# Query and key chunks turned by VectorE in 32x32 blocks instead of by TensorE, with tokens ordered by remainder modulo 4

## The reference, cut to what matters

```python
proj = x @ w_in                       # (256, 2048) @ (2048, 19456)
q_a, k_a, v_a, q_r, k_r, v_r, g_r, gate_a, gate_b = split(proj)
# A: 3 groups x 8 heads of 128, (window, dilation) = (128,1), (512,4), (2048,16)
#    rotary on the first 32 of 128 columns of q_a and k_a
#    query t attends to t, t-d, t-2d, ... inside the window; groups mixed by their softmax sums
# B: retention, 8 heads, qk width 128, v width 256, rotary on all 128 columns,
#    decay per head, norm per head, swish gate g_r
y = (sigmoid(gate_a) * (o_a @ w_branch_attn) + sigmoid(gate_b) * (o_r @ w_branch_ret)) @ w_out
x = layer_norm(alpha * x + y)
# 32 experts in 4 groups: top group, then top 2 SwiGLU experts of it (2048 -> 512 -> 2048)
x = layer_norm(alpha * x + moe(x))
```

## Time and profile before

| | us |
|---|---|
| median of 3 runs (2060.63 to 2063.73) | 2062.45 |
| profiled execution, span from first to last instruction | 2058.1 |
| PE busy / DVE busy / ACT busy in the span | 1766.7 / 994.9 / 757.1 |

### The profile page before, as it was taken

How to read it: one execution, slowest core, us unless ns; L and a number is a source line. 1 busy time by engine, 2 the same in 40 slices (tenths; PEclk the granted TensorE clock), 3 DMA queues, 4 the chain that set the end, 5 groups by cost and what they waited for, 6 DMA issues and landing times.

```text
span 2058.1 us, 25311 instructions
## 1 busy us (share of the span) xinstructions
PE 1766.7 (86%) x9868; PEld 1141.9 (55%) x9868; DVE 994.9 (48%) x1469; ACT 757.1 (37%) x1321; POOL 15.3 (1%) x34
## 2 busy tenths in 40 slices
PE   9999999999999999999999986666566666666667
PEld 7888888888888888888888541111112111111222
DVE  5454454555444444566565564334433433343357
ACT  5444444344444444354443422222222222222221
POOL 0000000000000000000000000000000000000000
PEclk9999999999999999999999988887888888887888
DMA  7556655455556555467677999999999999999998
GB/s 247 194 175 189 199 175 176 150 184 187 191 181 194 172 185 178 155 188 238 218 279 287 381 428 425 429 431 429 427 430 433 430 426 429 431 430 427 430 428 367
DMA packets 139042, 615.07 MB, mean 299 GB/s; under 512 B 14228, under 2 KB 14900, under 8 KB 117840
## 3 DMA queue, kind: packets, MB, share of 16 engines
q1 hardware_dynamic: 138240, 611.75, 77.5%
q0 software_dynamic: 720, 2.18, 0.6%
HBM read 609.61 MB, written 2.36 MB: 297 GB/s over the span
## 4 chain that ended last, share of the span: by engine, by line
PE 54%; DMA 33%; issue 10%; DVE 2%; ACT 0%; SPq 0%; DVEq 0%; POOL 0%; POOLq 0%
DMA W<-in_w_expert_up_dram 21%; PE PS L593 14%; PE PS L595 14%; PE PS L594 14%; DMA W<-in_w_expert_down_dram 11%; PE PS L1173 5%; PE PS L1224 2%; PE PS L962 1%; PE PS L1314 0%; PE PS L1129 0%; DVE ZACC L2234 0%; PE PS L1052 0%; DMA VC<-VS 0%; PE PS L1295 0%; PE PS L939 0%
## 5 line engine op out<-in xcount | busy, mean ns | idle before, releaser
L570 DVE TENSOR_TENSOR WL<-RAW,WH 128x1024 fp32r<-128x1024 f32 x384 | 457.4, 1221 | 403.9 <-ACT WH L566 402.5
L566 ACT ACTIVATE WH<-RAW 128x1024 fp32r<-128x1024 f32 x384 | 394.5, 1058 | 261.6 <-PE PS L595 199.8
L593 PE MATMUL PS<-WH,XH 128*128 128x512 f32 x1216 | 480.0, 395 | 0.1
L595 PE MATMUL PS<-WH,XL 128*128 128x512 f32 x1216 | 474.0, 390 | 0.0
L594 PE MATMUL PS<-WL,XH 128*128 128x512 f32 x1216 | 473.3, 389 | 0.0
L1173 PE MATMUL PS<-W,XE 128*32 128x512 f32 x2016 | 277.3, 698 | 135.0 <-DMA W<-in_w_expert_up_dram 133.6
L2234 DVE TENSOR_TENSOR ZACC<-PS,ZACC 128x1024 f32<-128x1024 f32 x124 | 146.0, 1219 | 294.3 <-PE PS L1295 294.3
L1224 PE MATMUL PS<-W,HT 128*32 128x512 f32 x992 | 171.0, 851 | 135.7 <-DMA W<-in_w_expert_down_dram 135.7
L593 PEld LDWEIGHTS PS<-WH,XH 128*128 128x128 f32 x1216 | 228.3, 188 | 49.3 <-issue 1.7
L595 PEld LDWEIGHTS PS<-WH,XL 128*128 128x128 f32 x1216 | 228.2, 188 | 48.3
L594 PEld LDWEIGHTS PS<-WL,XH 128*128 128x128 f32 x1216 | 228.6, 188 | 45.8
(11 more groups left out here) (333 smaller groups left out, 1472.7 us busy)
## 6 DMA issues: line engine op xcount, KB each, us to landing
RAW<-in_w_in_dram SPq DMA_DIRECT2D x304, 512.0 KB, 4.5
W<-in_w_expert_gate_dram SPq DMA_DIRECT2D x61, 2048.0 KB, 28.6
W<-in_w_expert_up_dram SPq DMA_DIRECT2D x61, 2048.0 KB, 33.0
W<-in_w_expert_down_dram SPq DMA_DIRECT2D x28, 4096.0 KB, 35.2
RAW<-in_w_branch_ret_dram SPq DMA_DIRECT2D x32, 512.0 KB, 5.2
RAW<-in_w_out_dram SPq DMA_DIRECT2D x32, 512.0 KB, 6.0
W<-in_w_expert_down_dram SPq DMA_DIRECT2D x7, 2048.0 KB, 30.4
RAW<-in_w_branch_attn_dram SPq DMA_DIRECT2D x16, 512.0 KB, 5.3
```

Source lines behind the costliest of these rows:

```text
L566: act.activation(WH[:, i % RING], RAW[:, i % RING], ACT.Copy).then_inc(hi_done, 1)
L570: dve.tensor_tensor(WL[:, i % RING], RAW[:, i % RING], WH[:, i % RING].bitcast(F32), ALU.subtract).then_inc(lo_done, 1)
L593: pe.matmul(PS[:, bank + t], hs, wh, start=first and j == 0, stop=False)
L595: mm = pe.matmul(PS[:, bank + t], ls, wh, start=False, stop=end)
```

## The change

Query and key chunks are no longer transposed by PE and read by ACT. DVE transposes NAT itself: for each of the four groups of 32 partitions of NAT (a) and each of the four groups of 32 head columns (b) one instruction turns 32 partitions by 256 elements (2 token tiles x 4 heads x 32 columns) straight into QT, KTT, QRT or KRT; 16 instructions a chunk, four at each of the steps READ+2 to READ+5 (q_a, k_a) or READ+4 to READ+7 (q_r, k_r). The group of four waits for a drain and, in the second half, for scores long done. ACT reads the next chunk into NAT when the 16 are done.

So that a group of 32 partitions holds the tokens of one remainder modulo 4, tokens stand in a tile in the order given by `turn`: high_x and low_x write XH and XL permuted, positions are loaded by four DMAs, one for each remainder, the masks, decays and triangle are permuted on the host, and read_turn (heads alone) and read_merged put the order right again. QT of group 0 and KRT are laid out with the heads innermost, so that DVE writes them with a distance of 4 and of 8 elements, and PE loads weights from them with the same distances. move_values issues four DMAs of 64 KB where it issued one of 256 KB.

```diff
 LAG = 2
-V_MOVES = (NG - 1) * TOK
...
 RET_AT = [123 + 5 * h for h in range(HH)]
-EARLY_ROTS = [c for c in ROTS if CHUNKS[c][0] in ("qa", "ka")]
-TURNS = sorted([(READ[c] + 3 + (0 if c in EARLY_ROTS else 3 * t), "chunk", c, t) for c in ROTS for t in range(TOK)]
-               + [(ATT_AT[h] + 13, "head", h, 0) for h in range(HH)])
+TURNS = [(ATT_AT[h] + 13, h) for h in range(HH)]
 NT = len(TURNS)
...
     t = np.arange(P)
+    turn = CLASSES * (t % ROWS) + t // ROWS
...
         q = CLASSES * (t[:, None] % CM) + member
         for g, (window, dilation) in enumerate(GROUPS):
-            k = np.arange(SEQ)[None, :] if g == 0 else CLASSES * np.arange(CM)[None, :] + member
+            k = np.concatenate([turn, P + turn])[None, :] if g == 0 else CLASSES * np.arange(CM)[None, :] + member
...
             col += ok.shape[1]
     first[:, C_ID:C_ID + P] = np.eye(P)
-    first[:, C_TRI:C_TRI + P] = t[:, None] <= t[None, :]
...
-    n = (np.arange(TOK)[None, :] * P + t[:, None]).astype(np.float64)
+    n = (np.arange(TOK)[None, :] * P + turn[:, None]).astype(np.float64)
...
+    QT = at("QT", 96, [NG, QD, HH, TOK, ROWS])
+    KTT = at("KTT", 108, [NG, QD, HH, TOK, ROWS])
...
-    KRT = at("KRT", 136, [HH, SEQ])
+    QRT = at("QRT", 132, [QD, HH, TOK, ROWS])
+    KRT = at("KRT", 136, [QD, HH, TOK, ROWS])
     VR = at("VR", 140, [2, TOK, CH])
...
-                            sp.dma_start(POSI[:], positions.rearrange("b (t p) -> p (b t)", p=P),
-                                         allow_slow_non_contiguous=True).then_inc(pos_landed, 16)
+                            for r in range(CLASSES):
+                                sp.dma_start(POSI[r * ROWS:(r + 1) * ROWS],
+                                             positions.rearrange("b (t m r) -> r m (b t)", m=ROWS, r=CLASSES)[r],
...
                 pe.wait_ge(sums_read, half * NP + PLAIN.index(c) + 2)
+        q_near = QT[:, 0].rearrange("p a h t m -> p (a h t m)").rearrange("p (n h) -> p n h", h=HH)
+        k_ret = KRT[:].rearrange("p a h t m -> p (a h t m)").rearrange("p (n t h) -> p n t h", t=TOK, h=HH)
+
         def att_scores(half, h):
-            pe.wait_ge(turn_read, half * NT + turn_index("chunk", 2 * NG - 1, 1) + 2)
+            pe.wait_ge(qk_turned, len(ATT_ROTS) * (half + 1))
             if h:
                 pe.wait_ge(o_norm, half * HH + h)
             for u in range(TOK):
-                pe.matmul(PS[:, S0 + u, 0:SEQ], QT[:, 0, h, u * P:(u + 1) * P], KTT[:, 0, h], start=True, stop=True)
+                pe.matmul(PS[:, S0 + u, 0:SEQ], q_near[:, TOK * u * CM:TOK * (u + 1) * CM, h],
+                          KTT[:, 0, :, h].rearrange("p a t m -> p t a m"), start=True, stop=True)
             for u in range(TOK):
                 for g in range(1, NG):
                     c0 = SEQ + (g - 1) * CM
                     for c in range(P // CM):
-                        own = slice(u * P + c * CM, u * P + (c + 1) * CM)
-                        mm = pe.matmul(PS[c * CM:(c + 1) * CM, S0 + u, c0:c0 + CM], QT[:, g, h, own], KTT[:, g, h, own],
+                        r = P // CM * u + c
+                        mm = pe.matmul(PS[c * CM:(c + 1) * CM, S0 + u, c0:c0 + CM], QT[:, g, r, h], KTT[:, g, r, h],
                                        start=True, stop=True)
             mm.then_inc(scored, 1)
...
             if h == 0:
                 pe.wait_ge(o_norm, half * HH + HH)
             else:
                 pe.wait_ge(r_masked, half * HH + h)
-            pe.matmul(PS[:, S0, 0:SEQ], KRT[:, h, 0:P], QRT[:, h, :], start=True, stop=True)
-            pe.matmul(PS[:, S0, SEQ:SEQ + P], KRT[:, h, P:SEQ], QRT[:, h, P:SEQ], start=True,
+            pe.matmul(PS[:, S0, 0:SEQ], k_ret[:, :, 0, h], QRT[:, :, h].rearrange("p a t m -> p t a m"),
+                      start=True, stop=True)
+            pe.matmul(PS[:, S0, SEQ:SEQ + P], k_ret[:, :, 1, h], QRT[:, :, h, 1], start=True,
                       stop=True).then_inc(r_scored, 1)
         def ret_values(half, h):
...
-            bank = turn_bank(kind, a, t)
-            pe.wait_ge(turn_read, half * NT + n + (0 if bank == S0 else 1))
-            if bank == S0 and half:
-                pe.wait_ge(r_masked, HH)
-            if kind == "chunk":
-                pe.wait_ge(rotated, half * len(ROTS) + ROTS.index(a) + 1)
-                for h in range(HH):
-                    mm = pe.transpose(PS[:, bank, h * P:(h + 1) * P], NAT[:, t, h * DH:(h + 1) * DH], ident)
-            else:
-                pe.wait_ge(o_norm, half * HH + a + 1)
-                for u in range(TOK):
-                    mm = pe.transpose(PS[:, TB, u * P:(u + 1) * P], ON[:, u], ident)
+        def turn(half, h):
+            pe.wait_ge(turn_read, half * HH + h)
+            pe.wait_ge(o_norm, half * HH + h + 1)
+            for u in range(TOK):
+                mm = pe.transpose(PS[:, TB, u * P:(u + 1) * P], ON[:, u], ident)
             mm.then_inc(turned, 1)
         for half in range(2):
...
         def high_x(b):
             act.wait_ge(x_turned, b + 1)
-            act.activation(XH[:, 2 * b:2 * b + 2].rearrange("p k n -> p (k n)"), PS[:, 2 + b % X_BANKS],
+            act.activation(XH[:, 2 * b:2 * b + 2].rearrange("p k (t r m) -> p (k t) r m", r=CLASSES, m=ROWS),
+                           PS[:, 2 + b % X_BANKS].rearrange("p (x m r) -> p x r m", m=ROWS, r=CLASSES),
                            ACT.Copy).then_inc(x_high, 1)
...
                 if before and before[-1] in ROTS:
-                    act.wait_ge(turned, half * NT + turn_index("chunk", before[-1], 1) + 1)
+                    if before[-1] in ATT_ROTS:
+                        act.wait_ge(qk_turned, half * len(ATT_ROTS) + ATT_ROTS.index(before[-1]) + 1)
+                    else:
+                        act.wait_ge(r_turned_in, half * len(RET_ROTS) + RET_ROTS.index(before[-1]) + 1)
                 elif before:
                     act.wait_ge(g_used, half * len(GRS) + GRS.index(before[-1]) + 1)
                 if kind == "gr":
...
                                scale=0.5).then_inc(sums_read, 1)
-        def read_turn(half, n, kind, a, t):
-            act.wait_ge(turned, half * NT + n + 1)
-            if kind == "head":
-                dst = OT[:, half * HH + a].rearrange("p (m r) -> p r m", r=CLASSES)
-                src = PS[:, TB, 0:SEQ].rearrange("p (r m) -> p r m", r=CLASSES)
-            else:
-                kd, g, _, _ = CHUNKS[a]
-                buf = {"qa": QT[:, g], "ka": KTT[:, g], "qr": QRT, "kr": KRT}[kd]
-                dst = buf[:, :, t * P:(t + 1) * P]
-                src = PS[:, turn_bank(kind, a, t)].rearrange("p (h n) -> p h n", h=HH)
-                if kd == "qa" or (kd == "ka" and g):
-                    part = P // CLASSES
-                    dst = buf.rearrange("p h (r m) -> p h r m", r=CLASSES)[:, :, :, t * part:(t + 1) * part]
-                    src = PS[:, turn_bank(kind, a, t)].rearrange("p (h m r) -> p h r m", h=HH, r=CLASSES)
-            act.activation(dst, src, ACT.Copy).then_inc(turn_read, 1)
+        def read_turn(half, h):
+            act.wait_ge(turned, half * HH + h + 1)
+            act.activation(OT[:, half * HH + h].rearrange("p (t r m) -> p r t m", r=CLASSES, m=ROWS),
+                           PS[:, TB, 0:SEQ].rearrange("p (r t m) -> p r t m", r=CLASSES, m=ROWS),
+                           ACT.Copy).then_inc(turn_read, 1)
         def att_exp(half, h):
             act.wait_ge(masked, half * HH + h + 1)
...
         def read_merged(j, t):
             act.wait_ge(m_turned, TOK * j + t + 1)
-            act.activation(MT[:, 4 * j:4 * j + 4, t * P:(t + 1) * P],
-                           PS[:, S0 + t].rearrange("p (b n) -> p b n", b=4),
+            act.activation(MT[:, 4 * j:4 * j + 4, t * P:(t + 1) * P].rearrange("p b (m r) -> p b r m", r=CLASSES),
+                           PS[:, S0 + t].rearrange("p (b r m) -> p b r m", b=4, r=CLASSES),
                            ACT.Copy, scale=0.5).then_inc(m_read, 1)
         def merged_high(q):
...
         def low_x(b):
             dve.wait_ge(x_high, b + 1)
-            dve.tensor_tensor(XL[:, 2 * b:2 * b + 2].rearrange("p k n -> p (k n)"), PS[:, 2 + b % X_BANKS],
-                              XH[:, 2 * b:2 * b + 2].rearrange("p k n -> p (k n)").bitcast(F32),
-                              ALU.subtract).then_inc(x_low, 1)
+            low, high = (s[:, 2 * b:2 * b + 2].rearrange("p k (t r m) -> p (k t) r m", r=CLASSES, m=ROWS)
+                         for s in (XL, XH))
+            dve.tensor_tensor(low, PS[:, 2 + b % X_BANKS].rearrange("p (x m r) -> p x r m", m=ROWS, r=CLASSES),
+                              high.bitcast(F32), ALU.subtract).then_inc(x_low, 1)
         def rotate(half, c, step):
...
             if step == (0 if attend else 2):
                 dve.tensor_tensor(nat[:, :, :, 0:2 * n], nat[:, :, :, 0:2 * n], tmp[:, :, :, 0:2 * n],
-                                  ALU.add).then_inc(rotated, 1)
+                                  ALU.add)
+
```

(87 more changed lines are left out.)

1 line of the change is left out of this document (removed).

## The result

The changed kernel takes 2073.25 us (median of 4 runs, 2072.12 to 2074.84) against 2063.09 us of the kernel before beside it: 10.2 us slower, ratio 1.0052 with a 95% interval of 1.0040 to 1.0063. The profiled execution has a span of 2072.9 us. I had forecast 2055.0 us, 7.4 us faster.

The account below looks back on a forecast made before the run. PE was taken to bound the projection, the weight stream the experts. -14.3 + 0.3 + 3 + 1 + 2.1 + 0.5 = -7.4 us, so 2062.45 - 7.4 = 2055.0 us; range 2046 to 2082.

Parts of the forecast that it names:

- the sign that the prediction had named: In the projection: the prediction called itself wrong if PE idles more than 10 us there.
- Removed from PE, 14.3 us: Projection's q and k chunks: PE's dropped transposes save 0.90 us per group of eight, 0.44 per four, all on the path.
- The distance in the writes, 3 us: QT of group 0 and KRT, 4 of 16 chunks: strided DVE writes cost 0.8 us a chunk, 2 for k_r; 3 taken.
- The price of a transpose, x = 0.35: DVE in q and k chunks: 0.35 us from one transpose's start to the next, bounded by 0.28 and 0.85.
- the 0.53 that the sum gave: DVE in each chunk: transposes are in time up to x = 0.53 us; beyond, a chunk costs 16 (x - 0.53).
- At the second head: Steps 85 and 86, q_r's transposes beside the mask: 0.3 us of room at tile 87; 0.3 us lost for both halves.
- The move of the values, 2.1 us: PE's wait for the moved values: eight DMA issues for two, 1.4 us waiting per half, 2.1 us more in all.
- The bound of 7.1: PE's wait for the moved values: 7.1 us more if the DMAs take the longest landing.
- Weights with a distance, 1 us: PE's loads of near queries and retention keys: 0.07 us more each, 4.5 us if all showed, most hidden; 1 taken.
- Start, 0.5 us: Kernel start: four position DMAs on SP delay tile 4's weight load by 1 to 2 us; 0.5 us, 2 at worst.
- MT's reading: ACT, under edits at nothing: MT written four apart, 0.45 us more for each of 8, where ACT is not full.
- DVE becomes the bound: Rival for q and k chunks, deciding from x = 0.53 us: 2098 us at 0.62, about 2065 at 0.55; chance 0.24.

Follow-up runs that it names:

- the later head: The changed kernel with the first attention head of each half two steps later (67 for 65): 2063.49 us, ratio 1.0011 to the kernel before.

## Why the prediction was wrong

The time of 2073.25 us lies inside the range of 2046 to 2082, but the change made the kernel slower and not faster, and the sign that the prediction had named came: PE idles 17.1 us in the projection, more than 10. The range was wide for the rival of a DVE that is the bound of every chunk, so that it held the time owes something to luck. By its own steps, with what the landmarks give:

- **Removed from PE, 14.3 us: right.** The kernel without distance gives 5.2 and 5.4 us for the six attention chunks of a half (5.4 forecast). In the second half without transposes the four groups of four give 1.9 us (1.76 forecast).
- **The distance in the writes, 3 us: the step that failed.** The mechanism was named and weighed at 0.23 us by ACT's row; the chip gives 0.64 - 0.44 = 0.20 at four elements and 0.23 at eight. But the distance was added to x = 0.35. With x = 0.44 as it is, the near transposes start 0.64 us apart: 16 x 0.11 = 1.8 us a chunk, not 0.8. The landmark gives 2.5. What is left lies in the same sum: a subtraction between transposes takes 1.26 us to the next start (38.54 to 39.85, 42.41 to 43.67), not 1.16, and PE loses 0.1 us more behind each stop (its next product starts 0.34 us later instead of 0.23). DVE is done with tile 15 at 55.1 us and PE starts it at 55.19, where 52.6 was the deadline. The two waits of 0.82 and 0.85 us show only part of this. Near queries 2 x 2.5 = 5.0 us; k_r 2 x 3.2 = 6.4 (from the second head to the third the changed kernel loses 3.1 and 3.3 us, the kernel without distance nothing), where I had 0.8 and 2 a chunk and took 3 for all four; together 11.4 for 3.
- **The price of a transpose, x = 0.35.** One takes 0.437 us and the next starts 0.445 later: they don't overlap, as the subtractions of the earlier trace rows do. I took a value near the stream's spacing where the single duration of the earlier trace rows (0.426) was the nearer row. The bounds had held it, and at chunks without distance 0.44 stays under the 0.53 that the sum gave. At the second head it doesn't fit: 8 (0.445 - 0.30) - 0.3 = 0.9, and the landmarks give 1.7 us a half, 3.4 for 0.3. PE stops there at tile 87 and again at the next; what makes up the rest no run separates.
- **The move of the values, 2.1 us.** The waits are 2.34 and 3.12 us, 5.1 by landmarks net of the old one. An issue takes 0.50 us instead of 0.55 and the median landing 3.6 instead of 5.3, but the slowest (6.4 us for 6.7) hardly got shorter with the transfers, and PE waits for the last of all; I had taken the shortest of the old ones. The bound of 7.1 held.
- **What no step had:** the clock at 0.50 behind the longer of the two waits, 2.7 us; the rsqrt that starts a microsecond late behind the longer run of moves, 2.0 us.
- **Weights with a distance, 1 us:** 319 to 336 ns for 188, an excess of 0.13 to 0.15 us a load where the earlier trace rows had suggested 0.07; by landmarks 0.06 us a head in attention and about 0.12 in retention, 1.4 us. Most of it is hidden, as said.
- **Start, 0.5 us:** 0.2. MT's reading takes 1090 ns for 594 and is hidden, as said.

-14.3 + 11.4 + 3.4 + 5.1 + 2.7 + 2.0 + 1.4 + 0.2 = 11.9 us, against 11.5 by the trace. Most of these terms are read from the same traces that they add up to; what tests them are the experiments: 9.6 us with the moves undone for the 9.8 of move, clock and rsqrt, 13.3 us without distances (both with the later head) for the 12.8 of writes and loads, 1.7 us in the second half without q_r's transposes. The largest part of the 19 us between forecast and trace is the distance, 8.4 us; the second head has 3.1, the move 3.0, and 4.7 were in no step. The timed medians say 10.2; two executions' expert stretches differ by a few microseconds.

The rival "DVE becomes the bound" had the place right (PE waiting for WL) and 0.53 us as the point of decision, but in four chunks of sixteen only, and by the distance. Its price of 43 us was for all. The Trainium skill ("VectorE: DVE Perf Modes", the three transpose paths), by which I had estimated 0.62 us for 256 columns, is not borne out: 0.44. The Trainium skill ("SBUF — State Buffer", the note on cachelines), cited for the writes, has fp32 free up to a distance of four; DVE's transposes take about 0.63 for 0.44 us at four and 0.67 at eight, and PE's weight loads 319 for 188 ns. The measurement decides: a distance of four is not free here.

## What to carry to other kernels

When work moves from a full engine to a half idle one, price it where the idle engine has a deadline: room in steps, not in totals. A layout that leaves a distance between elements is paid twice, by who writes and by who reads; look for the order of dimensions in which both are runs before accepting it (here 10 us slower became 3.5 us faster). And a DMA cut into four small ones costs four issues, and the slowest of them landed no sooner than one of the large (6.4 against 6.7 us): ask what waits for the last of them.

## What was not expected of the hardware

PE idle for 3.12 us was followed by almost 6 us of work at a granted clock of 0.50; idle for 2.34 us it was not, and with nine products put into the wait neither. But the kernel without distance fell to 0.50 as well, for about 3 us, after a wait of 2.41 us, where 2.46 us in its first half did nothing; so the length of the wait alone does not decide it, and what else does was not tried. Its eight products take 2.05 us where 1.13 is the rule:

```profile
667.63 2.05 PE L912 MATMUL PS<-VA,PT 128*128 128x128 f32 x8 [2.41 <-DMA VC<-VS]
```

GpSimd's first rsqrt after sixteen DMA issues comes 1.47 us behind its addition, after four it comes 0.49 us behind; with a power operation done in between there is no such gap.
